# The attention's output products for the first half of the tokens, moved into the attention's last slots, and the first six weight splits, moved to VectorE

## The reference

```python
h = rms_norm(x, norm_mix[l])
proj = h @ w_in[l]
aq, ak, av, rq, rk, rv, rg, ga, gr = jnp.split(proj, offsets, axis=-1)
att = sliding_window_attention(...)          # 8 heads, window of 128
ret = retention_chunkwise(...)               # 4 heads, chunks of 128 tokens
ret = head_group_norm(ret, ret_gn_gain[l]).astype(x.dtype) * jax.nn.silu(rg)
merged = jax.nn.sigmoid(ga) * (att @ w_att_o[l]) + jax.nn.sigmoid(gr) * (ret @ w_ret_o[l])
x = x + merged @ w_out[l]
```

## Time and profile before

| | |
|---|---|
| median of three runs | 2699.96 us (2686.93 to 2701.96) |
| the profiled execution | 2698.87 us, span 2697.1 us |
| mean granted clock of TensorE | 0.989 |
| TensorE, matmuls | 2643.2 us, 98% |
| VectorE | 1544.2 us, 57% |
| ScalarE | 1026.3 us, 38% |
| GpSimd | 1180.5 us, 44% |

### The profile page before, as it was taken

The page is one execution under the profiler, slowest core; times in us unless marked ns, Lnnn a source line. Parts: engine busy times, 40 slices in busy tenths (PEclk is TensorE's granted clock), DMA queues, the critical chain, the costliest instruction groups (busy, mean ns, idle before and its releaser), DMA issues.

```text
span 2697.1 us, 35511 instructions
## 1 busy us (share of the span) xinstructions
PE 2643.2 (98%) x13170; PEld 2215.7 (82%) x13170; DVE 1544.2 (57%) x2628; ACT 1026.3 (38%) x2053; POOL 1180.5 (44%) x936
## 2 busy tenths in 40 slices
PE   7999999999999999999999999999999999999998
PEld 7788888777888888888888778989978888878886
DVE  4325555675335554454798641157647666668787
ACT  4122333574223422232444621057634322244443
POOL 2347877344325565555232763234234444300205
PEclk9999999998999999999999999979999999999999
DMA  4555766705552222221752344233143333273524
GB/s 171 183 183 198 266 229 233 263 1 171 188 181 76 72 86 86 78 79 64 287 184 94 118 167 157 59 65 64 24 141 98 106 107 112 94 257 132 188 94 164
DMA packets 161465, 372.35 MB, mean 138 GB/s; under 512 B 21349, under 2 KB 42469, under 8 KB 157669
## 3 DMA queue, kind: packets, MB, share of 16 engines
q1 hardware_dynamic: 161294, 370.08, 40.2%
HBM read 267.94 MB, written 101.83 MB: 137 GB/s over the span
## 4 chain that ended last, share of the span: by engine, by line
PE 87%; DVE 4%; POOL 3%; DMA 2%; ACT 2%; issue 2%; SPq 0%; POOLq 0%; DVEq 0%; ACTq 0%
PE PS L793 12%; PE PS L795 12%; PE PS L796 12%; PE PS L847 5%; PE PS L849 5%; PE PS L848 5%; PE PS L625 4%; PE PS L627 4%; PE PS L626 4%; PE PS L948 3%; PE PS L609 3%; PE PS L610 3%; PE PS L611 3%; PE PS L926 1%; PE PS L738 1%
## 5 line engine op out<-in xcount | busy, mean ns | idle before, releaser
L2128 POOL TENSOR_TENSOR WL<-WRAW,WH 128x512 fp32r<-128x512 f32 (+1 forms) x149 | 252.1, 1693 | 360.8 <-ACT WH L997 360.8
L793 PE MATMUL PS<-HH,WL 128*128 128x512 f32 (+1 forms) x928 | 349.1, 376 | 5.1 <-DVE HS L1770 3.1
L796 PE MATMUL PS<-HH,WH 128*128 128x512 f32 (+1 forms) x928 | 347.5, 374 | 0.0
L795 PE MATMUL PS<-HL,WH 128*128 128x512 f32 (+1 forms) x928 | 347.4, 374 | 0.0
L1453 DVE TENSOR_TENSOR WL<-TS,WH 128x512 fp32r<-128x512 f32 x216 | 226.9, 1060 | 184.3 <-ACT WH L997 184.1
L847 PE MATMUL PS<-WH,DAL 128*128 128x512 f32 x756 | 295.5, 391 | 6.0 <-DVE WL L1728 6.0
L848 PE MATMUL PS<-WL,DAH 128*128 128x512 f32 x756 | 294.9, 390 | 0.0
L849 PE MATMUL PS<-WH,DAH 128*128 128x512 f32 x756 | 294.8, 390 | 0.0
L2323 POOL TENSOR_TENSOR X<-X,DV 128x512 f32<-128x512 f32 x56 | 90.1, 1634 | 358.6 <-DVE DV L1840 275.7
L997 ACT ACTIVATE WH<-TS 128x512 fp32r<-128x512 f32 x216 | 130.9, 623 | 203.2 <-POOL TS L2144 203.1
L793 PEld LDWEIGHTS PS<-HH,WL 128*128 128x128 f32 x928 | 174.6, 188 | 36.9 <-DVE HS L1770 3.3
(11 more groups left out here) (371 smaller groups left out, 6172.9 us busy)
## 6 DMA issues: line engine op xcount, KB each, us to landing
WRAW<-in_u_f SPq DMA_DIRECT2D x56, 512.0 KB, 3.6
WRAW<-in_u_in SPq DMA_DIRECT2D x54, 512.0 KB, 4.4
WRAW<-scr_t SPq DMA_DIRECT2D x52, 512.0 KB, 3.7
scr_h<-HS SPq DMA_DIRECT2D x96, 256.0 KB, 2.1
WRAW<-in_u_gu SPq DMA_DIRECT2D x44, 512.0 KB, 3.5
scr_t<-TTa SPq DMA_DIRECT2D x19, 1024.0 KB, 4.1
WRAW<-in_u_out SPq DMA_DIRECT2D x24, 512.0 KB, 3.5
scr_x<-X SPq DMA_DIRECT2D x24, 512.0 KB, 5.0
```

Of the source, the lines that this page charges most:

```text
L793: e.matmul(PS[:, b, 0:wd], wl[:, blk(kk)], op_moving(q, kk, c0, wd, 0), start=(kk == 0), stop=False)
L795: e.matmul(PS[:, b, 0:wd], wh[:, blk(kk)], op_moving(q, kk, c0, wd, 1), start=False, stop=False)
L796: mm = e.matmul(PS[:, b, 0:wd], wh[:, blk(kk)], op_moving(q, kk, c0, wd, 0), start=False, stop=(kk == 3))
L2128: e.tensor_tensor(lo, raw, hi.bitcast(F32), ALU.subtract).then_inc(*c.inc("w_lo_p", i))
```

## The change

It has two parts.

In the opening, SP loads the identity behind the second tile of x. VectorE, not GpSimd, takes the low parts of the first six units. VectorE and ScalarE do unit 0 and tile 1's parts ahead of tile 2's norm, and the transposes of tiles 2 to 7 stand one product later.

At the end of the slots, the `ao` products are ordered half by half (`AOG`), and the first six, all of tokens 0 to 511, stand one each at the end of slots 32 to 37, on TensorE and on VectorE. The other ten follow the slots. The retention's gates are ordered half by half (`GATED`), gate i beside product i+6, and the last six gates without one. `RO2` takes tiles 0 to 5 of the first half before those of the second. The gate tiles `TA` become eight half tiles, four of them loaded once retention step 23 is done, and `TA`, `RG` and `TB` have other addresses.

```diff
-    TA = at("TA", [P, 2, S], MI + 18)
-    RG = at("RG", [P, 4, 512], MI + 9.5)
-    TB = at("TB", [P, 2, 512], MI + 5.5)
+    TA = ([at(f"TAa{i}", [P, 512], B2 + 16 + 2 * i) for i in range(4)]
+          + [at(f"TAb{i}", [P, 512], MI + 18 + 2 * i) for i in range(4)])
+    RG = [at(f"RG{i}", [P, 512], MI + kb) for i, kb in enumerate((9.5, 11.5, 1.5, 3.5))]
+    TB = at("TB", [P, 2, 512], MI + 13.5)
...
-            return n % 2 == 0 or order[n][0] == "u_out2"
+            return n > 5 and n % 2 == 0 or order[n][0] == "u_out2"
...
+    N_TAIL = LAG_A + 3
+    AOG = [(n, half) for half in range(2) for n in range(8)]
...
+    GATED = [(j, half) for half in range(2) for j in range(8)]
+    RO2 = [(n, half) for half in range(2) for n in range(6)] + [(n, half) for half in range(2) for n in range(6, 8)]
...
-            if i < 6:
-                back(1, 2 + i)
+            if 1 <= i < 7:
+                back(1, 1 + i)
...
+        def att_out(i):
+            n, half = AOG[i]
+            w.wait_ge(*bk.out(("apv", n1 - 1 if half else n1 // 2 - 1)))
+            proj_t(("ao", n, half), U["u_ao", n // 2], half, ATH, ATL, 4, (n % 2) * 512)
...
+            if s >= n1:
+                att_out(s - n1)
...
         w.wait_ge(*bk.out(("apv", n1 - 1)))
-        for n in range(8):
-            for half in range(2):
-                proj_t(("ao", n, half), U["u_ao", n // 2], half, ATH, ATL, 4, (n % 2) * 512)
+        for i in range(N_TAIL, 16):
+            att_out(i)
...
+        first_square(0)
+        first_square(1)
+        back(1, 0)
+        split()
+        back(1, 1)
+        first_square(2)
+        split()
+        first_square(3)
...
+            j, half = GATED[i]
             w.wait_ge(*c.at("rg_m", i))
             e.activation(RH[:, j, hs(half)], QK[:, j, hs(half)], ACT.Copy).then_inc(*c.inc("rg_h", (j, half)))
-            feed(("ao", j, half))
+            if i + N_TAIL < 16:
+                feed(("ao", *AOG[i + N_TAIL]))
...
+        norm(1, 0, GB[:, :])
+        norm(1, 1, GB[:, :])
+        back(1, 0)
+        split(0)
+        back(1, 1)
+        norm(1, 2, GB[:, :])
+        split(1)
+        norm(1, 3, GB[:, :])
         for i, (j, lo, wd) in enumerate(OPEN):
-            if i < 4 and not on_pool(2 + i):
+            if i < 4:
...
+            key = "ao", *AOG[i]
+            w.wait_ge(*bk.full(key))
+            w.wait_ge(*gate_in(i))
+            if i < 2:
+                w.wait_ge(*bk.out(("rs", nr - 1)))
+                w.wait_ge(*c.at("r_q", nr - 1))
+            else:
+                w.wait_ge(*c.at(f"m1_{i % 2}", i - 2))
+            e.tensor_tensor(TB[:, i % 2, :], PS[:, bk.at(key), :], gate_at(i)[:, :], ALU.mult).then_inc(*bk.free(key))
...
+            n, half = GATED[i]
             w.wait_ge(*c.at(f"lga{i % 4}", ("rg", i)))
             e.scalar_tensor_tensor(out=QK[:, n, hs(half)], in0=QK[:, n, hs(half)], scalar=GAIN[:, n:n + 1],
-                                   in1=RG[:, i % 4, :], op0=ALU.mult, op1=ALU.mult).then_inc(*c.inc("rg_m", i))
-            key = "ao", n, half
-            w.wait_ge(*bk.full(key))
-            w.wait_ge(*c.at(f"lg{n % 2}", ("ga", n)))
-            if i >= 2:
-                w.wait_ge(*c.at(f"m1_{i % 2}", i - 2))
-            e.tensor_tensor(TB[:, i % 2, :], PS[:, bk.at(key), :], TA[:, n % 2, hs(half)],
-                            ALU.mult).then_inc(*bk.free(key))
-            feed(key)
+                                   in1=RG[i % 4][:, :], op0=ALU.mult, op1=ALU.mult).then_inc(*c.inc("rg_m", i))
+            if i + N_TAIL < 16:
+                att_out(i + N_TAIL)
+                feed(("ao", *AOG[i + N_TAIL]))
...
-        e.dma_start(ID[:, :], a["c_id"]).then_inc(*c.inc("c_id", 0, 16))
-        e.dma_start(X[:, 0, :], a["x"][0]).then_inc(*c.inc("x0", 1, 16))
-        e.dma_start(GB[:, :], bcast(a["norm_mix"], D)).then_inc(*c.inc("gb0", 1, 16))
-        for t in range(1, NT):
+        for t in range(NT):
             e.dma_start(X[:, t, :], a["x"][t]).then_inc(*c.inc(f"x{t}", 1, 16))
-            if t <= NRAW:
+            if t == 0:
+                e.dma_start(GB[:, :], bcast(a["norm_mix"], D)).then_inc(*c.inc("gb0", 1, 16))
+            if t == 1:
+                e.dma_start(ID[:, :], a["c_id"]).then_inc(*c.inc("c_id", 0, 16))
+            if 1 <= t <= NRAW:
...
+        w.wait_ge(*bk.full(("ro", 4 * 5 + 3)))
+        w.wait_ge(*bk.full(("rst", 4 * 5 + 3)))
         for i in range(4):
-            load_rg(i)
-        w.wait_ge(*bk.out(("as", len(A1) - 1)))
-        for n in range(2):
-            load_ga(n)
+            load_ga(i)
         for i in range(16):
-            n, half = i // 2, i % 2
+            if i == 1:
+                w.wait_ge(*bk.full(("ro", nr - 1)))
+                load_rg(0)
+                load_rg(1)
+            if i == 3:
+                w.wait_ge(*bk.full(("rot", nr - 1)))
+                load_rg(2)
+                load_rg(3)
+            n, half = AOG[i]
             w.wait_ge(*bk.out(("ao", n, half)))
             e.dma_start(scr_ga[n][:, hs(half)], TB[:, i % 2, :]).then_inc(*c.inc(f"m1_{i % 2}", i, 16))
-            if half == 1 and n + 2 < 8:
-                load_ga(n + 2)
             if i + 4 < 16:
-                w.wait_ge(*c.at("rg_m", i))
-                load_rg(i + 4)
-            feed(("ao", n, half))
+                w.wait_ge(*bk.out(("as", n1 - 1)))
+                load_ga(i + 4)
+            if i >= N_TAIL:
+                if i - N_TAIL + 4 < 16:
+                    w.wait_ge(*c.at("rg_m", i - N_TAIL))
+                    load_rg(i - N_TAIL + 4)
+                feed(("ao", n, half))
+        for i in range(16 - N_TAIL, 12):
+            w.wait_ge(*c.at("rg_m", i))
+            load_rg(i + 4)
```

More of the change, by code:

```diff
@@ L446, in in0_place, with gate_at, gate_in @@
         return scr[tile - base][:, hs(int(q[0]) - 1)]
+    def gate_at(i):
+        return TA[i if i < 4 else 4 + i % 4]
+    def gate_in(i):
+        return c.at(("lg0", "lg1", "lm0", "lm1")[i % 4], ("ga", i))
     def queries_in(t):
@@ L474, in build @@
     EARLY_SLOTS = {"P5": 0, "P2": 1, "P4": 2}
+    N_TAIL = LAG_A + 3
+    AOG = [(n, half) for half in range(2) for n in range(8)]
     A2 = [(h, i) for h in range(8) for i in range(NT)]
     OPEN = [(j, 0, 256) for j in range(4)] + [(j, 256, 256) for j in range(4)] + [(j, 512, 512) for j in range(4)]
-    RO2 = [(n, half) for n in range(6) for half in range(2)] + [(n, half) for half in range(2) for n in range(6, 8)]
+    GATED = [(j, half) for half in range(2) for j in range(8)]
+    RO2 = [(n, half) for half in range(2) for n in range(6)] + [(n, half) for half in range(2) for n in range(6, 8)]
     PO = [0, 4, 1, 5, 2, 6, 3, 7]
@@ L1027, in act_program, with first_square @@
         e.activation(SM[:, 23:24], HALF, ACT.Square)
[L1028 to L1031, removed]
+        def first_square(tt):
             w.wait_ge(*c.at(f"x{tt}", 1))
             square(1, tt, SS[0][:, tt:tt + 1])
+        first_square(0)
[6 more added lines that the diff above has]
+        first_square(3)
         for i, (j, lo, wd) in enumerate(OPEN):
@@ L1041, in act_program @@
                 feed(key)
-            if i < 6:
-                back(1, 2 + i)
+            if 1 <= i < 7:
+                back(1, 1 + i)
             if i < 4:
-                w.wait_ge(*c.at(f"x{4 + i}", 1))
-                square(1, 4 + i, SS[0][:, 4 + i:5 + i])
+                first_square(4 + i)
         for half in range(2):
@@ L1480, in norm @@
                                    op1=ALU.mult).then_inc(*c.inc("n_x", (k, tt)))
[L1482 to L1488, removed]
+        w.wait_ge(*c.at("gb0", 1))
+        norm(1, 0, GB[:, :])
[6 more added lines that the diff above has]
+        norm(1, 3, GB[:, :])
         for i, (j, lo, wd) in enumerate(OPEN):
-            if i < 4 and not on_pool(2 + i):
+            if i < 4:
                 split(2 + i)
@@ L2174, in pool_program @@
         w.wait_ge(*c.at("half", 0))
-        for tt in range(4):
-            if tt >= 2 and on_pool(tt - 2):
-                split(tt - 2)
+        for tt in range(NT):
             rsqrt(1, tt, VV[0][:, tt:tt + 1], RR[0][:, tt:tt + 1])
-        for i, (j, lo, wd) in enumerate(OPEN):
-            if i < 4 and on_pool(2 + i):
-                split(2 + i)
-            n_split[0] = max(n_split[0], min(3 + i, 6))
-            if lo == 512:
-                feed(("aq", j, 1))
-            if i < 4:
-                rsqrt(1, 4 + i, VV[0][:, 4 + i:5 + i], RR[0][:, 4 + i:5 + i])
+        n_split[0] = 6
+        for j in range(4):
+            feed(("aq", j, 1))
         for half in range(2):
@@ L2252, in pool_program @@
         for i in range(16):
-            j, half = i // 2, i % 2
+            j, half = GATED[i]
             w.wait_ge(*c.at("rg_h", (j, half)))
```

14 lines of the change are left out of this document (8 added, 6 removed).

## The result

| | before | after |
|---|---|---|
| median (runs) | 2699.12 us (20; 2685.95 to 2704.35) | 2674.33 us (20; 2671.08 to 2689.42) |
| profiled execution, span | 2697.1 us | 2672.4 us |
| mean granted clock | 0.989 | 0.996 |

What follows compares the result with a forecast made beforehand. TensorE, busy 98% of the span, was taken as the bound, so only its waits and half clock could be won. Opening 3.3 + slots' end 10.0 + `RL` 0.9 = 14.2 us, from 2698.87 to 2684.7 us; range 2677 to 2693.

Steps and rivals of the forecast that it cites:

- The opening: Start of the kernel: the new order lets TensorE's first product begin at 14.9 us, 3.3 us earlier.
- The tightest margin: Opening, first product of tokens 256 to 511: wanted at 30.7 us, tile 3 finished at 30.4, margin 0.3 us.
- the cost sum for VectorE: Opening: three more low parts cost VectorE 3.7 us, two faster norms save 4.2 us, load up to tile 7 as before.
- the rival in which slow norms make TensorE wait: Opening: norms still take 3.4 us twice, TensorE waits 3.4 us for tile 3; saving 10.8, 2688.1 us; chance 0.11.
- The slots' end: From slot 32: six products fill 4.6 us of waits and avoid 5.4 us lost at half clock, 10.0 us won.
- The rival of longer slots: Slots' end: products lengthen the slots' chain, the clock falls, 27.8 us more against 14.2 won; 2712.5 us; chance 0.04.
- The rival in which TensorE stops for the merging loads `MG`: After the slots: `MG` still waits for gate 15, everything but the opening is given back; 2695.6 us; chance 0.05.
- The wait for RL: Ahead of the first `ro2` product: TensorE's 1.7 us wait shrinks to 0.8, so 0.9 us won.
- the extra weight unit: Output products' stage: one more 512 KB fetch, 1.7 us, and ro4's 2.4 us low part could delay `RL`.
- the range: Whole kernel: eight in ten for a time of 2677 to 2693 us.
- two thirds of 0.60: Main forecast, chance 0.60, own range 2681 to 2689 us; about two thirds lies below the 2686.5 us limit for faster.
- all of 0.08: Better case, chance 0.08: opening's first product also reaches full clock earlier, no `RL` wait stays; 2680 us.

Runs made afterwards that it cites:

- GpSimd's version: Changed kernel with step 4's second-attention scores formed twice and `AVT` copies first, plus low parts of units 0, 2 and 4 back on GpSimd: 2671.14 us.
- the kernels with `AVT` first: Changed kernel with VectorE's `AVT` copies ahead of its sums: 2670.40 us; with step 4's scores of the second attention also formed twice: 2670.87 us.
- before with doubled scores: The kernel before with the scores of step 4 of the second attention formed twice, nothing else: 2687.92 us.
- with the groups removed: Before and changed kernel, each with step 4's scores of the second attention formed twice, so TensorE's `PT` wait is covered: 2687.92 against 2673.05 us.
- the products placed late: Changed kernel with step 4's scores doubled and `AVT` copies first, its six products moved to slots 34 (two), 35, 36 and 37 (two): 2672.15 us.

## Where the prediction was right, and where not, step by step

**The opening.** Each step landed within 0.15 us: the gain at 6.35 (0.43 us sooner, 0.4 said), unit 0's low part at 12.23 (12.3), TensorE at 14.80 (14.9), tile 3 done at 30.49 (30.4), 512 columns at 46.20 (46.1). Two things behind it were off. The tightest margin was 1.1 us, not 0.3: TensorE reached that product at 31.56, not 30.7, since I took its first products at 2.9 us each and they ran at 0.21 us a matmul until 20.7. And the cost sum for VectorE (3.7 us taken on, 4.2 saved) was right but decided little, as GpSimd's version shows; the rival in which slow norms make TensorE wait had no ground, because with GpSimd at the roots alone no norm took more than 1.29 us.

**The slots' end.** 10.0 us was said for the waits and the half clock; slot 32 to the end of the six products takes 645.22 - 617.19 = 28.0 us, where 27.8 was said. With the wait for `RL` it is 11.2 us where 10.9 was said. No wait above 0.2 us, clock 1.00. The rival of longer slots had no wait to start from. The rival in which TensorE stops for the merging loads `MG` falls as well: from the first `ro2` product to the wait for `PT` it is 1075.1 us before and 1076.3 after, so nearly all that was won was kept.

**The wait for RL.** Gate 7's `RL` was done at 672.74 us; 673.1 was said, and TensorE asked at 672.59. The wait is 0.20 us, not 0.8, and in the kernels with `AVT` first, where TensorE comes at 668.5 to 669.0, there is none. So `RL` comes earlier with TensorE. The 673.1 were reckoned from a slot 32 at 618.91, though, and it came 1.7 us earlier. Counted from product 6's multiply on VectorE (648.14 us), `RL` took 24.6 us, where 23.6 was taken over from before: 1.0 us more, where my sum took 1.6 of up to 4.1 for the extra weight unit. Between that multiply and this `RL` GpSimd now does the low parts of two units (at 649.48 for 2.75 us and at 666.51 for 2.38), and did none there before; beside the first of them a gate's multiply on VectorE took 2.88 us instead of 0.74. What each costs is not parted. TensorE's ten products took 27.4 us, not 27.2. So the term was mis-sized by 0.6 us, and this lies within what the wait does by itself: in the three traces with before's slots it is 1.1, 1.7 and 2.6 us.

**Where no term stood.** 1.7 us go behind `AVT` where the clock falls. It fell in all four profiles of kernels with the slots' part and this wait, and in none of the three without the slots' part; with one execution each, that isn't enough to say whether the slots' part or chance decides. And TensorE's wait for `HLF` (0.3 us in before's profile) is 0.6 to 1.5 us in the others, that of before with doubled scores among them, so it isn't the change's.

**The number.** 2684.7 us was the profiled time less 14.2, and the profiled time was one of the upper group. As a difference 14.2 is right (14.9 measured with the groups removed). As a time it lands where the changed kernel's upper group is (2686.3), while its median (2674.33) is of the lower one, 2.7 us below the range; the mean of its runs, 2677.8, is within it. Where a single number lands against these medians is luck, since it hangs on how many of the runs are upper ones. The step that failed is "the median of the runs shown is 1.1 us higher, well inside their spread, and I leave the number there": the three runs shown were 2686.93, 2699.96 and 2701.96, a gap of 13 us that I took for spread, and the 27 us at clock 0.50 behind 1762 us that make it stood in the same trace. I looked at the clock only where the change is. A slip stands in the chances too: two thirds of 0.60 and all of 0.08 make 0.48 for faster, not 0.51.

## What to carry to other kernels

Before a forecast is set against a median, look at all of the runs: where they lie in two groups, find the stretch of lower clock that makes the gap, and forecast for each group. A wait of TensorE is worth its length and what the clock does behind it; filling it with real work of a later stage, or even with a repeated matmul, takes both away. And the place of an instruction in its engine's order was worth more here than which engine does it: what stands ahead of the first product decides, what is slower behind it mostly does not.

## What the runs showed of the hardware

- The same wait of about 1.06 us was followed by half clock in three of six traces and by full clock in three, and the stretch cost 13.6 to 15.4 us, over ten times the wait. Waits of 1.06, 0.78 and 0.69 us within five microseconds left the clock at 1.00 in the execution profiled. The Trainium skill (TensorE: Matmul & The Clock Gate, "Loop structure matters more than you think") shows the drop with a wait of 8 us ahead of every matmul; here one of an eighth of that, ahead of a single group, was enough some of the time.
- Behind an idle start the matmuls of 256 columns began every 0.21 us and then every 0.12 us, and the change of pace came 2.9 to 5.9 us after the first product (17.8 and 20.7 us), though the product began at the same time; the granted clock reads 1.00 in both stretches. It moves everything behind it by 1.3 us. One trace suggests what the slow pace is: with the products placed late, the pace was 0.12 us from the first product (14.83 us) to 15.9 and then 0.21 us to 19.2, and there the granted clock reads 0.50. So the 0.21 us of the other traces may be half clock too, which their record of the clock misses; that is argued from this one trace, not shown.
- A VectorE norm beside a GpSimd low part took 3.38 and 3.40 us against 1.28. A VectorE low part with only one operand in SBUF took 0.69 us there, the same as without GpSimd.
